# Moving the weight buffers of a two-block fp32 kernel to other SBUF addresses

## What is computed

```python
u = rmsnorm(h, g);  z = u @ w_in                       # block 1
a = dilated_window_attention(q, k, v)                  # 12 heads of 64
p = pool_branch(pz, w_grp, scale)                      # trailing means, grouped map
h = h + (sigmoid(ga) * (a @ w_att_out) + sigmoid(gp) * (p @ w_pool_out)) @ w_out
h = h + square(relu(rmsnorm(h) @ w_mlp_in)) @ w_mlp_out
x = rmsnorm(h)                                         # block 2 begins
y_att = neighbourhood_attention(q, k, v, rpb) @ w_att_o
y_rec = ((rg_lru_fwd(u) + rg_lru_bwd(u)) * gelu(y)) @ w_rec_o
x = x + (sigmoid(g_att) * y_att + sigmoid(g_rec) * y_rec) @ w_out
out = rmsnorm(x + square(relu(rmsnorm(x) @ w_ff1)) @ w_ff2)
```

## Time and profile before

| | |
|---|---|
| median of 3 runs | 2854.98 us (2853.58 to 2857.79) |
| time of the profiled execution | 2853.58 us |
| its span, first to last instruction | 2851.7 us |
| TensorE busy | 2817.6 us, 99% of the span |
| TensorE's weight loads busy | 2268.1 us, 80% |
| VectorE, ScalarE, GpSimd busy | 1701.1, 1314.5, 179.1 us |
| mean granted clock of TensorE | 0.996 of full speed |
| mean busy share of the DMA engines over the span | about 31% (the queues' 30.0, 0.5 and 0.2%) |

### The profile page before, as it was taken

One profiled execution on the slowest core, in us unless ns is written; L12 is line 12 of the kernel. 1 busy time (PEld: TensorE's weight loads), 2 busy tenths in 40 slices (PEclk: granted clock), 3 DMA queues, 4 the chain that ended last, 5 costly groups with the idle time before them and its releaser, 6 DMA issues.

```text
span 2851.7 us, 34547 instructions
## 1 busy us (share of the span) xinstructions
PE 2817.6 (99%) x13096; PEld 2268.1 (80%) x13096; DVE 1701.1 (60%) x2462; ACT 1314.5 (46%) x2129; POOL 179.1 (6%) x133
## 2 busy tenths in 40 slices
PE   8999999999999999999999999999999999999998
PEld 6777777888888888887777788777888888888886
DVE  4333365335866667688555523888345866667786
ACT  4444452114555554444345413788123655544452
POOL 1222420000000000000122200000000000000000
PEclk9999999999999999999999999999999999999998
DMA  3111111123334465532311111121114343385441
GB/s 126 38 31 36 45 38 45 54 64 119 136 148 151 156 260 212 167 118 78 128 52 52 45 52 59 52 60 52 52 42 158 128 160 148 137 302 185 155 133 70
DMA packets 86123, 302.71 MB, mean 106 GB/s; under 512 B 9552, under 2 KB 9680, under 8 KB 79696
## 3 DMA queue, kind: packets, MB, share of 16 engines
q1 hardware_dynamic: 84672, 295.88, 30.0%
q10 hardware_dynamic: 1296, 4.72, 0.5%
HBM read 225.07 MB, written 75.50 MB: 105 GB/s over the span
## 4 chain that ended last, share of the span: by engine, by line
PE 96%; DVE 2%; issue 1%; ACT 1%; DMA 0%; POOL 0%; POOLq 0%; SPq 0%; DVEq 0%; ACTq 0%
PE ps L402 24%; PE ps L2406 16%; PE pa L2708 11%; PE ps L2708 11%; PE ps L2737 9%; PE pa L2737 9%; PE pa L402 3%; PE ps L2755 2%; PE ps L2584 2%; PE pa L2511 2%; PE pa L2483 2%; PE pa L2492 1%; PE pa L2456 1%; PE pa L2584 0%; PE ps L2418 0%
## 5 line engine op out<-in xcount | busy, mean ns | idle before, releaser
L392 DVE TENSOR_TENSOR w_lo<-w_raw,w_hi 128x1024 fp32r<-128x1024 f32 x134 | 159.7, 1191 | 418.4 <-ACT w_hi L386 418.4
L386 ACT ACTIVATE w_hi<-w_raw 128x1024 fp32r<-128x1024 f32 x134 | 137.8, 1029 | 390.0 <-PE ps L402 266.0
L402 PE MATMUL ps<-a_hi,w_hi 128*128 128x512 f32 x896 | 277.4, 391 | 0.8 <-DVE a_lo L1707 0.8
L402 PE MATMUL ps<-a_lo,w_hi 128*128 128x512 f32 x896 | 276.1, 389 | 0.0
L402 PE MATMUL ps<-a_hi,w_lo 128*128 128x512 f32 x896 | 276.0, 389 | 0.0
L2406 PE MATMUL ps<-a_hi,w_hi 128*128 128x512 f32 x672 | 225.2, 416 | 9.5 <-DVE a_lo L1655 9.5
L1171 ACT ACTIVATE krh<-k_rraw 128x512 fp32r<-128x512 f32 x192 | 121.0, 630 | 234.0 <-PE ps L2737 108.9
L2406 PE MATMUL ps<-a_lo,w_hi 128*128 128x512 f32 x672 | 214.5, 400 | 0.0
L2406 PE MATMUL ps<-a_hi,w_lo 128*128 128x512 f32 x672 | 214.2, 400 | 0.0
L1935 DVE TENSOR_TENSOR krl<-k_rraw,krh 128x512 fp32r<-128x512 f32 x192 | 132.5, 690 | 132.6 <-ACT krh L1171 132.2
L402 PEld LDWEIGHTS ps<-a_hi,w_hi 128*128 128x128 f32 x896 | 167.2, 188 | 39.7 <-issue 2.5
(11 more groups left out here) (348 smaller groups left out, 5945.9 us busy)
## 6 DMA issues: line engine op xcount, KB each, us to landing
w_raw<-wstream SPq DMA_DIRECT2D x134, 512.0 KB, 3.5
k_rraw<-hff SPq DMA_DIRECT2D x224, 256.0 KB, 2.8
hff<-hbuf SPq DMA_DIRECT2D x32, 1024.0 KB, 3.9
wA<-wff SPq DMA_DIRECT2D x16, 2048.0 KB, 8.6
hff<-hbuf SPq DMA_DIRECT2D x32, 768.0 KB, 3.3
w_raw<-wff SPq DMA_DIRECT2D x32, 512.0 KB, 4.2
f_raw<-wff SPq DMA_DIRECT2D x32, 512.0 KB, 4.5
hres<-zt SPq DMA_DIRECT2D x16, 512.0 KB, 2.6
```

Of the source, the lines that this page charges most:

```text
L386: nc.scalar.activation(w_hi[:, slot, 0:n], w_raw[:, slot, 0:n], ACT.Copy).then_inc(s_whi, 1)
L392: nc.vector.tensor_tensor(w_lo[:, slot, 0:n], w_raw[:, slot, 0:n], w_hi[:, slot, 0:n].bitcast(F32), ALU.subtract).then_inc(s_wlo, 1)
L402: mm = nc.tensor.matmul(out[0:m, c], w[0:kp, slot, wofs:wofs + m], x[0:kp, k, c * HC:(c + 1) * HC], start=first and n == 0, stop=last and ...
```

## The change

Regions are laid out in another order. W, which lay between G and Z, now lies behind T. The gap after Z shrinks from 256 to 64 bytes.

```diff
@@ build
         A0 = base
         B0 = A0 + 64 * KB
         G0 = B0 + 64 * KB
-        W0 = G0 + 32 * KB
-        Z0 = W0 + 24 * KB
-        T0 = Z0 + 8 * KB + 256
-        C0 = T0 + 16 * KB + 64
+        Z0 = G0 + 32 * KB
+        T0 = Z0 + 8 * KB + 64
+        W0 = T0 + 16 * KB + 64
+        C0 = W0 + 24 * KB
```

## The result

The changed kernel takes 2891.03 us (median of 4 runs, 2889.14 to 2893.9) against 2854.33 us before: a ratio of 1.0131, 95% interval 1.0117 to 1.0145. It is 36.7 us slower, far outside the forecast of 2850 to 2860 us. The profiled execution took 2893.31 us, some 2 us above the median, against 2853.58 us before, so the two traces lie 39.7 us apart and the medians 36.7 us.

What follows compares the result with a forecast made beforehand. TensorE's pace of 226.7 ns a matmul was taken as the bound. TensorE 0, ScalarE and VectorE 0 and DMA 0 left the profiled 2853.6 us unchanged, so the forecast median was 2855.0 us, range 2850 to 2860 us.

Steps and rivals of the forecast that it cites:

- What bounds the kernel: Whole kernel: TensorE, busy 99% of the span and 96% of the chain, at one pace of 226.7 ns a matmul.
- TensorE reading W and T, cost taken 0: Long matmuls: weight loads take 188 ns from every region, covered by the matmul in front, so moving W and T costs 0.
- The pace rows: Chain pieces from L402, L2708, L2737 and L2755, all giving 226.7 ns a matmul with operands in different regions.
- The bound on the bad side: L2737: if weight loads from T took 261 ns, 2304 matmuls would cost 34 ns more each, 79 us in all.
- ScalarE, VectorE, DMAs, gaps: 0: Other engines and transfers on moved tiles: cost 0, at most 1.6 us exposed work and 0.5 us DMA; no new waits.
- Rows 5 and 6: Profile rows of ScalarE and VectorE work, such as copies of 630 and 598 ns, cited to show starts play no part.
- Clock dips: Near 1356 us the clock halves, costing about 4.8 us; a run with one less or more: 2850.2 or 2859.8 us, chance 0.10.
- Faster by alignment: L2737: moving operands starting at a multiple of 256 save 32 periods each, 30.7 us, giving 2824.3 us; chance 0.03.
- Slower by weight loads from T: L2737: loads of `klh` and `kll` from 192 past outgrow their cover; 2886 us at 240 ns, 2934 at 261; chance 0.03.
- The sentence on what would make me wrong: SBUF speed depending on an unvaried address bit: a start at a multiple of 256, or engines' accesses meeting; look in L2737.
- no change: Whole kernel: measured time stays within 0.2%, 5.7 us, of the time before; chance 0.90.

Runs made afterwards that it cites:

- the two maps: Matmul-only kernels on one large buffer, no other engine at work: one varied operand starts, the other also widths, steps and neighbours; 226.7 ns a matmul at distance 0, 512 columns.
- first map: Separate kernel of 110 sections of 48 matmuls from one buffer, no other engine working; only operand starts varied; 226.7 ns at distance 0, 234.4 ns at 96 bytes.

## Why the prediction was wrong

The change costs 36.7 us because it broke an equality that nobody had written down: before, weights and moving operands of all long matmuls started at the same remainder of 256 bytes. The changed kernel has W 128 bytes off A, B and G, and T 192 bytes off W. About 7670 matmuls take weights from W (L402, L2406, L2418, L2584, four of seven slots of L2708, two of eight of L2755), and 2304 in L2737 pair T with W. The latter cost 5.1 us (2304 x 2.2 ns, and 2.6 + 2.5 us in the table by stage), the former then have the rest of the 36.7 us, some 31.6 us or 4.1 ns each on average (by the traces, 34.6 of 39.7 us): 5.7 to 6.7 ns where they follow each other undisturbed, less in the attention stages, which lost only 1.5 and 3.1 us.

By the steps of the prediction:

- *What bounds the kernel.* Right. TensorE's pace is the bound, and a loss of 6 ns in a matmul is a loss in time.
- *TensorE reading W and T, cost taken 0.* This is the step that failed. I argued from the duration of weight loads, 188 ns in every region. They are still 188 ns, at a pace of 233 as at 226.7, so this row says nothing about the pace. The pace rows could not speak either: the operands had the same starts in all four stages. I wrote that down as unknown, and then took the value of the rows that cannot vary. What the runs showed in its place is 2.2 to 7.6 ns more for a matmul whose two operands start apart, in the stages with weights in W as much as in L2737.
- *The bounds.* The bound on the bad side counted only L2737. The weights in W, three times as many matmuls, stood in none of the bounds. 7670 x 6.7 ns + 2304 x 6.7 ns = 67 us is what 233.3 ns everywhere would give, and the slowest layout that was run lost 60 us.
- *ScalarE, VectorE, DMAs, gaps: 0.* Right, each. Rows 5 and 6 did not move by more than 1 ns, and no wait was added. The median landing of a transfer into `w_raw` is 3.5 us in both pages although its rows now start at a multiple of 256 bytes; the Trainium skill's rule on split descriptors (DMA: Bandwidth & Descriptors, "How a descriptor splits into AXI transactions") is not seen in the time, whose digits (0.1 us) would just show 3%.
- *Clock dips.* Of no account: the spread within a set of runs, 2 to 7 us, is far below the loss.
- *The rivals.* "Faster by alignment" was wrong in sign: nothing in the two maps went below 226.7 ns at 512 columns. "Slower by weight loads from T" had the sign but neither mechanism nor place: the loads didn't grow, and 86% of the loss (31.6 of 36.7 us) is outside L2737. The sentence on what would make me wrong was near the cause, with "a speed of reading or writing SBUF that depends on an address bit the rows above do not vary", but neither form that it gave is what was found. A start at a multiple of 256 costs nothing by itself (226.7 ns with everything moved by 128 bytes), and no VectorE and no DMA is needed beside TensorE's two reads (first map). Nor did that case have a chance of its own. With a 0.90 on "no change", that was the real error: rows that could not vary had been counted as evidence.

What is open is the mechanism. The maps show that the starts of TensorE's own two operands are enough, with a period of 256 bytes, and that history counts near distance 0. Whether the two are read at the same time and meet in some part of the partition was not shown, and the results with other widths and with alternating distances do not fit a simple loss for each clash. The Trainium skill (SBUF — State Buffer, section "SBUF: two separate sides") says that contention on the engine side comes only from the port pair that VectorE and GpSimd share, and that TensorE never waits for anyone. In the first map no other engine was at work, so nobody else is to blame here either; but TensorE's rate still fell by 3%, and whoever takes that sentence to mean that addresses are free for TensorE can lose 60 us in this kernel (the layout with W moved by 96 bytes).

No layout was found that beats the kernel before. It already has distance 0 in all its long matmuls, and 226.7 ns is the quickest pace of the maps.

## What to carry to other kernels

Treat a shift of a tile as an edit that can cost time. Where matmuls follow each other without gaps, let weights and moving operand start at the same remainder of 256 bytes, and at multiples of 32. This is shown for 128x128 weights and 512 moving columns; at 256, 448 and 480 columns distance 64 was the quicker one (117.8, 202.2 and 216.0 ns against 120.0, 206.7 and 216.7), so measure other widths. Padding a region to keep equal starts is cheap, here 192 bytes in each of two gaps against 37 us. To find such a loss, divide pieces of the chain by their matmuls and compare stages: neither the busy share nor the duration of the weight loads shows it. And where all rows of a trace share a property that a change breaks, they bound nothing; give that case a chance.

## What the runs showed of the hardware

- Matmuls with 128x128 weights and 512 moving float32 columns at full clock follow each other at 226.7 ns or, with the operands' starts apart, at 228.9 to 234.4 ns, by the tables above. ScalarE and VectorE did not react to the changed layout beyond 1 ns (630, 598 and 1225 ns a piece), nor did the landing of transfers into `w_raw` (3.5 us).
- At distance 0, 256, 384, 496 and 512 columns take 120.0, 173.4, 220.0 and 226.7 ns. From 256 to 512 that is 106.7 / 256 = 0.417 ns a column, one period at 2.4 GHz, and 13.3 to 13.4 ns beyond the columns each time. Other widths do not fit this: 448 and 480 columns take 206.7 and 216.7 ns, 20.0 and 16.7 beyond, and 128 columns take 111.7 ns.
- The pace depends on what ran before: the same distance of 16 bytes ran at 226.7 or at 233.3 ns for 96 matmuls, by what came before it.
